# Pool rows, keys and two routings of the first token tile moved ahead of the second tile's work in a block with two expert layers

## The reference, cut to what matters

```python
def peer(h, wq, keys, u_tab, v_tab):          # per 128 tokens
    q = (hblk @ wq).reshape(128, 8, 2, 128)
    s = einsum('nhpd,hpkd->nhpk', q, keys)
    top_s, top_i = top_k(s, 16)                # two lists of 16 per head
    cand_s = top_s[:, :, 0, :, None] + top_s[:, :, 1, None, :]
    best_s, best_pos = top_k(cand_s, 16)       # idx: 16 experts per head
    gate = softmax(best_s)
    act = gelu(einsum('nd,nhkd->nhk', hblk, u_tab[idx]))
    return einsum('nhk,nhkd->nd', gate * act, v_tab[idx])

def mixer_pool(h, w_in, w_grp, scale, w_out):
    m = multiscale_pool(h @ w_in)              # a 256x256 band over tokens
    m = einsum('btgc,gce->btge', m, w_grp)
    return (m * scale) @ w_out
```

## Time and profile before

| what | value |
|---|---|
| median of 3 runs | 2202.29 us (2201.87 to 2202.67) |
| the profiled execution's own time | 2196.84 us |
| its span, first to last instruction | 2195.0 us |
| mean granted TensorE clock | 0.943 of full |
| busy: PE, DVE, ACT, POOL | 83%, 67%, 41%, 28% |
| read from HBM | 721.24 MB, 329 GB/s over the span |

### The profile page before, as it was taken

How to read it: one execution, slowest core, us unless ns; L and a number is a source line. 1 busy time by engine, 2 the same in 40 slices (tenths; PEclk the granted TensorE clock), 3 DMA queues, 4 the chain that set the end, 5 groups by cost and what they waited for, 6 DMA issues and landing times.

```text
span 2195.0 us, 21985 instructions
## 1 busy us (share of the span) xinstructions
PE 1816.2 (83%) x7101; PEld 1091.2 (50%) x7101; DVE 1466.8 (67%) x3029; ACT 897.5 (41%) x2357; POOL 618.9 (28%) x567
## 2 busy tenths in 40 slices
PE   4888999889978688888678787996798888877786
PEld 3757998788867344443323233354344443333222
DVE  6766956857776666767567767516666668677754
ACT  3446433524463333434334445312433344344433
POOL 1160000000000344434244343103354345443441
PEclk9889989989998899999899999998999899999999
DMA  9654758545563799999899999746899999999996
GB/s 367 265 198 145 262 196 306 177 171 211 202 220 116 316 371 418 418 421 421 338 402 421 421 421 421 319 172 256 362 416 419 419 421 421 421 421 421 421 422 251
DMA packets 114690, 723.76 MB, mean 330 GB/s; under 512 B 11504, under 2 KB 13344, under 8 KB 34064
## 3 DMA queue, kind: packets, MB, share of 16 engines
q0 software_dynamic: 74864, 540.30, 59.6%
q1 hardware_dynamic: 39712, 182.07, 22.7%
HBM read 721.24 MB, written 1.08 MB: 329 GB/s over the span
## 4 chain that ended last, share of the span: by engine, by line
PE 36%; DMA 31%; DVE 20%; ACT 6%; issue 5%; POOL 2%; SPq 0%; DVEq 0%; ACTq 0%; POOLq 0%
DMA X<-in_k_uv,EI 15%; PE PS L2129 14%; DMA Z<-in_k_uv,EI 9%; DMA W<-in_peer_wq 5%; PE PS L2106 5%; DVE junk L1809 4%; PE PS L1822 3%; PE PS L1823 3%; PE PS L1824 3%; DVE ACC L1429 3%; DVE WL L1445 3%; PE PS L1915 2%; ACT WH L999 1%; DMA W<-in_ada_w 1%; PE PS L2182 1%
## 5 line engine op out<-in xcount | busy, mean ns | idle before, releaser
L2129 PE MATMUL PS<-X,dg 128*128 128x512 f32 x1372 | 673.1, 626 | 176.2 <-ACT dg L999 175.4
L1809 DVE CUSTOM_DVE_ANT_0 junk<-H,X 128x1024 f32<-128x1024 f32 x343 | 419.6, 1223 | 254.0 <-DMA X<-in_k_uv,EI 247.0
L990 POOL DMA_INDIRECT X<-in_k_uv,EI x343 | 376.1, 1097 | 623.2 <-PE PS L2129 328.8
L2129 PEld LDWEIGHTS PS<-X,dg 128*128 128x128 f32 x1372 | 251.2, 195 | 553.3 <-ACT dg L999 345.6
L999 ACT ACTIVATE CF<-DOT 128x1 f32<-128x1 f32 x512 | 102.3, 200 | 588.7 <-DVE DOT L1809 588.2
L2129 PE MATMUL PS<-Z,dg 128*128 128x512 f32 x504 | 246.7, 622 | 38.3 <-ACT dg L999 38.2
L1809 DVE CUSTOM_DVE_ANT_0 junk<-H,Z 128x1024 f32<-128x1024 f32 x126 | 154.1, 1223 | 89.9 <-DMA Z<-in_k_uv,EI 86.7
L999 ACT ACTIVATE dg<-CP,CG 128x128 f32<-128x128 f32 x512 | 205.5, 401 | 17.3 <-PE PS L2129 0.6
L2129 PEld LDWEIGHTS PS<-Z,dg 128*128 128x128 f32 x504 | 92.6, 195 | 175.3 <-ACT dg L999 100.4
L1822 PE MATMUL PS<-XH,WH 128*128 128x256 f32 x592 | 176.2, 298 | 2.3 <-ACT XH L999 1.2
L990 POOL DMA_INDIRECT Z<-in_k_uv,EI x126 | 136.3, 1082 | 136.5 <-PE PS L2129 115.8
(11 more groups left out here) (312 smaller groups left out, 2626.8 us busy)
## 6 DMA issues: line engine op xcount, KB each, us to landing
W<-in_ada_w SPq DMA_DIRECT2D x56, 1024.0 KB, 5.1
Y<-in_ada_w SPq DMA_DIRECT2D x16, 1024.0 KB, 5.9
W<-in_k_win SPq DMA_DIRECT2D x16, 1024.0 KB, 5.1
W<-in_peer_wq SPq DMA_DIRECT2D x16, 1024.0 KB, 16.6
W<-in_k_ffi SPq DMA_DIRECT2D x13, 1024.0 KB, 5.4
Y<-in_k_ffi SPq DMA_DIRECT2D x9, 1024.0 KB, 4.9
W<-in_ffn_w_out SPq DMA_DIRECT2D x8, 1024.0 KB, 5.7
W<-in_ab_w_out SPq DMA_DIRECT2D x6, 1024.0 KB, 5.1
```

The lines of the kernel that those rows point to most:

```text
L990: e.indirect_dma_start(out=WS[k][:, :], out_offset=None, in_=I[f"k_uv{ly}"][:, :], in_offset=bass.IndirectOffsetOnAxis(ap=EI[t][:, j:j + 1 ...
L1809: e.tensor_tensor_reduce(junk, H[:, t, :], d[:, 0:D], 1.0, 0.0, ALU.mult, ALU.add, DOT[:, j:j + 1]).then_inc(v_dot, 1)
L2129: p = e.matmul(PS[:, 2 * t + q, :], dgb[n % 4][:, :], d[:, D + q * 512:D + (q + 1) * 512], start=(j == 0), stop=(j == 127))
```

## The change

What moves:

- Layer 1: the band, group and output products of the pool are split by tile. Tile 0's come first; tile 1's band follows, its `grp` and `po` stand behind the keys of heads 0 and 1, and its `rn`, `tt` and `h` behind the first experts. Layer 0: `rn` of tile 1 and `mod 9` change places with `tt` of tile 0.
- Both layers: chunks 0 to 3 of tile 0 come first, in banks 4 and 5, with the scores of heads 0 and 1 in bank 3. Heads 0 and 1 are routed one behind the other; tile 1's four chunks follow. The step without work at the end of each group goes.
- `experts` takes two steps behind each of the first 8 experts of tile 0.
- The pool's weight loads get eight slots of their own among the gather slots and stand ahead of everything else on SP; the gather ring has a new order. The gathers of layer 1 don't wait for the end of the pool any more, but for the slots they use.

```diff
-RING = list(range(2, 11)) + [13, 14, 15]
+RING = [9, 10, 4, 5, 3, 13, 2, 6, 14, 15, 7, 8]
...
-            b = bank(high)
+            b = 4 + i % 2 if (s4, hi) == (0, 128) else bank(high)
...
         if s4 == 0:
-            for lo in (0, 128):
-                for i in range(2):
-                    yield from chunk(i, lo, lo + 128)
-                if lo == 0:
-                    h00 = route(ly, 0, 0)
-                    next(h00)
-                    P("tt", ly, 1)
-                    yield from h00
-                    P("h", ly, 0)
-                    P("h", ly, 1)
-                    ready.add((ly, "h"))
+            for i in range(2):
+                yield from chunk(i, 0, 128)
+            h00 = route(ly, 0, 0)
+            next(h00)
+            for i in range(2, 4):
+                yield from chunk(i, 0, 128)
+            if ly:
+                for c in range(8):
+                    P("grp", c, 1, bank((1, 2)))
+                P("po", 1)
+            yield from h00
+            P("h", ly, 0)
+            ready.add((ly, "h"))
+            yield from route(ly, 0, 1)
+            if ly:
+                P("rn", ly, 1)
+                yield
+            P("tt", ly, 1)
+            yield
+            P("h", ly, 1)
+            for i in range(4):
+                yield from chunk(i, 128, 256)
+            return
...
-        yield
+        yield from route(ly, 0, 2 * s4 + 1)
...
             next(g, None)
+            if t == 0 and j < 8:
+                next(g)
...
     for ly in range(2):
-        P("rn", ly, 0)
-        if ly == 0:
+        if ly:
+            P("band", 0, 0, bank(low))
+            P("band", 1, 0, bank(low))
+            for c in range(0, 8, 2):
+                if c < 6:
+                    P("band", c + 2, 0, bank(low))
+                    P("band", c + 3, 0, bank(low))
+                P("grp", c, 0, bank(low))
+                P("grp", c + 1, 0, bank(low))
+            P("po", 0)
+            for c in range(8):
+                P("band", c, 1, bank((1, 2, 3)))
+            P("rn", ly, 0)
+        else:
+            P("ldq", ly, 0)
+            P("ldq", ly, 1)
+            P("ldk", ly)
+            P("rn", ly, 0)
+            P("rn", ly, 1)
             P("mod", 9, 0)
         P("tt", ly, 0)
-        P("rn", ly, 1)
...
-            P("ldp", 2)
-            P("ldp", 3)
+            for i in range(2, 10):
+                P("ldp", i)
+            P("ldq", 1, 0)
+            P("ldq", 1, 1)
+            P("ldk", 1)
...
-    rings = {"w": [0, 1, 2, 11, 12], "q": [0, 1], "p": [2, 6, 7, 8, 9, 10], "g": RING}
+    rings = {"w": [0, 1, 2, 11, 12], "q": [0, 1], "p": [3, 13, 14, 15, 7, 8, 9, 10], "g": RING}
...
-                    w.wait_ge(*arena(ly))
+                    w.wait_ge(p_part, 65)
+                    if ly and k in (4, 5):
+                        w.wait_ge(p_po, 1)
```

More of the change, by code:

```diff
@@ L417, in others @@
             yield from keys_part(ly, s4)
-            yield from route(ly, 0, 2 * s4 + 1)
         yield from between(ly)
@@ L498, in make_plan @@
             P("sc", 1)
[L499 to L507, removed]
     P("frn", 1)
@@ L545, in up @@
         return self.n
-NAME = {"xp": 3, "xt": 3, "mod": 2, "modp": 2, "gq": 3, "evac": 2, "rowp": 3, "rowa": 3, "pi": 4, "pie": 3, "band": 2, "grp": 2,
+NAME = {"xp": 3, "xt": 3, "mod": 2, "modp": 2, "gq": 3, "evac": 2, "rowp": 3, "rowa": 3, "pi": 4, "pie": 3, "band": 3, "grp": 3,
         "btp": 3, "bte": 3, "pqe": 5, "gate": 2}
@@ L850, in by_k, with scores @@
             return ap[:, :].rearrange("p (k n) -> p k n", k=k)
+        def scores(t, h):
+            return 3 if t == 0 and h < 2 else 7
         def arena(ly):
-            return (p_part, 65) if ly == 0 else (p_po, 1)
+            return (p_part, 65) if ly == 0 else (p_band, 16)
         def tt_done(name):
@@ L1291, in _ @@
                 elif kind == "band":
-                    c, b = a
-                    w.wait_ge(p_band, c + 1)
-                    act(mT[:, c, :], PS[:, b, 0:256], ACT.Copy).then_inc(a_band, 1)
+                    c, t, b = a
+                    w.wait_ge(p_band, 8 * t + c + 1)
+                    act(chunk(mT, c, t), PS[:, b, 0:128], ACT.Copy).then_inc(a_band, 1)
                 elif kind == "grp":
-                    c, b = a
-                    w.wait_ge(p_grp, c + 1)
-                    act(m2[:, c, :], PS[:, b, 0:256], ACT.Copy, scale=C2[:, c_psc + c:c_psc + c + 1]).then_inc(a_grp, 1)
+                    c, t, b = a
+                    w.wait_ge(p_grp, 8 * t + c + 1)
+                    act(chunk(m2, c, t), PS[:, b, 0:128], ACT.Copy, scale=C2[:, c_psc + c:c_psc + c + 1]).then_inc(a_grp, 1)
         @block.vector
@@ L2114, in _ @@
                     w.wait_ge(d_k, 16 * (ly + 1))
-                    take(7)
+                    b = scores(t, h)
+                    take(b)
                     for q in range(2):
                         c = 2 * h + q
-                        p = e.matmul(PS[:, 7, q * 128:(q + 1) * 128], chunk(PQ, c, t), KK[:, c, :], start=True, stop=True)
+                        p = e.matmul(PS[:, b, q * 128:(q + 1) * 128], chunk(PQ, c, t), KK[:, c, :], start=True, stop=True)
                     p.then_inc(p_rt, 1)
-                    free[7] = [(v_r7, nth("rt", ly, t, h, 2))]
+                    free[b] = [(v_r7, nth("rt", ly, t, h, 2))]
                 elif kind == "tail":
@@ L2154, in _ @@
                     take(b)
-                    for t in range(2):
-                        p = e.matmul(PS[:, b, 0:256], Z[:, t, c * 128:(c + 1) * 128], bd[:, c // 2, t, :], start=(t == 0),
-                                     stop=(t == 1))
+                    for i in range(2):
+                        p = e.matmul(PS[:, b, 0:128], Z[:, i, c * 128:(c + 1) * 128],
+                                     bd[:, c // 2, i, t * 128:(t + 1) * 128], start=(i == 0), stop=(i == 1))
                     p.then_inc(p_band, 1)
-                    free[b] = [(a_band, c + 1)]
+                    free[b] = [(a_band, 8 * t + c + 1)]
                 elif kind == "grp":
-                    c, b = a
+                    c, t, b = a
                     g = c // 2
```

45 lines of the change are left out of this document (21 added, 24 removed).

## The result

| | before | after |
|---|---|---|
| median, same chip | 2202.08 us (4 runs) | 2222.26 us (2218.56 to 2223.17, 4 runs) |
| profiled execution, its span | 2196.84, 2195.0 us | 2221.39, 2219.5 us |

The ratio is 1.0092 (95% interval 1.0074 to 1.0109): the change makes the kernel **20 us slower**. 2215 was forecast. On a second chip the changed kernel took 2225.21 us and the kernel before 2194.07 (ratio 1.0145, 1.0116 to 1.0174), 31 us more.

The account below looks back on a forecast made before the run. The DMA bounds the expert layers (512 gathers, 1275 us), with PE and DVE together as slow in the keys. Layer 0's +14.8 and layer 1's −1.5 sum to +13.3, told as 2215 us, range 2192 to 2228.

Parts of the forecast that it names:

- Slip of the first gather: Layer 0: rn of tile 1 and mod now precede tt, so the first gather starts 5.7 us later.
- Loads issued behind tile 1's last chunk, PE held 9.6: Layer 0, ahead of group 1: PE waits 9.6 us for query loads issued only then, holding tails and gathers behind it.
- Pause and lower clock: Layer 0, after PE's wait for loads: the DMA's rest lowers the granted clock to 0.50, costing 2.5 us (0 to 4).
- Rounds of 35.9, waits of 3.3: Keys: 35.9 us per 13 experts without the empty step; PE waits 3.3 us for second query loads in groups 2, 3.
- 92.9 gathers moved when the keys end: End of layer 0's keys (1002.2): 92.9 gathers moved against 101.4 before; the missing 8.5 cost 21.2 us, slip and pause included.
- The hole: Layer 0 at 1076 to 1096: DMA rest while tile 1's head 0 is late; earlier routing wins it, −10.2 us.
- Pool loads: End of layer 0: the early pool weight loads take DMA time from the last gathers, +3.8 us (bounds 0 to 8).
- Between the layers: Last tail of layer 0 to layer 1's first gather: splitting the pool by tile starts that gather 16.8 us earlier.
- Layer 1's keys: Layer 1, first gather to last tail: PE is held again by query loads; 15.3 us lost, leaving −1.5 for the layer.
- the prediction's own sign: Either layer: the prediction would be wrong if PE's wait for loads stayed under 5 us there.
- the keys aren't the limit: Keys of both layers: rounds go at the DMA's pace and 12 slots win the hold back; −8 us, 2194; chance 0.19.
- The rival of even shares: Query loads beside gathers: a load gets half the DMA, the four 3.3 us waits go; 2203, no change; chance 0.15.

Follow-up runs that it names:

- the fastest: Changed kernel with layer 0's keys in old order, two steps behind experts 116 to 127, six workless steps and 29 tails a group in layer 1: 2182.15 us.
- the kernel before without its hole: Kernel before, with two steps behind each of experts 116 to 127 of tile 0 in layer 0: 2187.16 us, ratio 0.996.
- The kernel with 29 tails: Changed kernel with six workless steps ahead of group 1, three more per later group, two steps for experts 112 to 127 of layer 0: 2190.88 us.
- eleven steps: 29-tail kernel with eleven workless steps for six ahead of group 1, layer 0's rn of tile 1 behind tt, double steps for experts 104 to 127: 2195.03 us.
- two kernels with later pool loads: Changed kernel with pool loads 4 to 9 held back until tail 251, or until tail 255: 2224.17 and 2227.14 us.
- layer 0's old order: Changed kernel with layer 0 up to its last routing in the order of the kernel before, early pool loads and ring kept: 2212.0 us.

## Why the prediction was right, and where it was off

The sign and the likeliest case came out: 2215 forecast, 2222 measured on that chip, and 13.3 of forecast loss stand against 24.5 between the profiled executions and 20.2 between the medians. The mechanism is the one forecast, PE held by query loads and too few tails in the keys. Its size in layer 0 was taken too small, and in layer 1 two terms were off that made up for each other.

- **Slip of the first gather, +5.7.** From the products ahead of layer 0 to the first gather the rows give 27.5 us with the change. With rn of tile 1 behind tt they give 21.5 (three kernels) or 23.5 (before and the fastest), so it costs 4 to 6. It doesn't show in the span, because the stages ahead of layer 0 ended 4.2 us earlier in this execution; their end lies anywhere between 695.6 and 703.1 in the executions of kernels with this order. Right.
- **Loads issued behind tile 1's last chunk, PE held 9.6.** The trace has 9.65 (8.60 on the second chip), until 776.97 and not 781.1. Right in size; but the runs show that its length is a poor measure of its cost. With four tails more ahead of it, 8.09 us of it were left and 11 us won.
- **Pause and lower clock, 2.5.** The clock's part is right: the granted clock was 0.50 (the lower of its two levels) at 776 to 782, PE's first product behind the hold took 3.75 us for 8 matmuls (1.99 at full clock), and the next tail 2.78 for 1.88, 2.7 in all. But the scores of head 2 came 18.1 us behind the hold, where 13.8 + 2.5 were forecast. The sum left out that ACT empties the first chunk before it makes the next diagonal, for which PE waited 1.32 us (until 786.35).
- **Rounds of 35.9, waits of 3.3.** 795.06 to 830.92 is 35.9; the waits were 2.90 and 2.25. The first two stretches from a group's scores to the next's took 77.1 and 74.6 us, forecast 75.1 each. Right.
- **92.9 gathers moved when the keys end.** This is the step that was mis-sized. Counted from each kernel's own first gather, 282 us on, the queue had moved 102.6 gathers before and 91.9 after: 10.7 fewer, 26.6 us (9.5 fewer on the second chip). The forecast's 21.2 less the slip are 15.5, so some 11 us were missed. Head 2's scores came 71.9 us behind the first gather, where 68.5 were forecast (1.6 for loads issued later, 1.8 behind the hold). By head 7's scores it was 261.8 for 254.6, so the groups took another 3.8 more. And 2.1 gathers were in flight at the end (94 issued, 91.9 moved) where 1.1 were taken, 2.5 us. That makes 9.7; the other 1.4 us stay open.
- **The hole, −10.2.** −8.3 (medians) and −8.7 (layer 0 of the profiled execution) in the kernel before without it. A little large.
- **Pool loads, +3.8.** 5.1 with only them, 6.7 in the fastest version. The forecast let 2.0 MB pass ahead of the last gather. 4.88 moved beside the last gathers, but holding six of the eight loads back gave only 1.1 us at the last gather, so the price is near that of the first two loads. "At most 8" held.
- **Between the layers, −16.8.** −14.5 and −15.9. Right: from the last tail's end (1439.76) to the start of rn (1484.90) the pool took 45.1, as forecast, with rn, turning, chunks and routing behind. In the chunks PE ran part of the time at the lower clock, so the first gather came 2 us later than forecast.
- **Layer 1's keys, 15.3 lost again.** 16.3 and 19.8. Right in the sum, in part by luck. The hold there was forecast at 6.5 us and measured 2.06 and 0.60. The loads of group 1 were issued 52.3 us behind the first gather and not 49.7, during chunks in which a tail came only every 7 us (1557.33, 1564.11), and a tail stood ahead of group 1. Head 2's scores then came 72.2 us behind the first gather, forecast 71.7, and 92.9 gathers had moved 276.5 us on, forecast 93.9. By the prediction's own sign ("under 5 us in a layer") the waits of layer 1 pass only if those of all groups are added, 6.3 us.

The rival "the keys aren't the limit" is half right, and that is the most useful miss. "In the keys PE and DVE together are as slow as the DMA" holds for 13 tails a round, but it isn't a limit: a round has room for one or two tails more at 0.4 us each (58 tails in 154.2 us, 52 in 151.7). The change took the empty step away and gave the heads a lead of 16 to 31 experts in layer 0. The kernel with 29 tails has leads of 10 to 18 there and keeps the DMA busy; the rest of the lead is tails not done. The rival of even shares is out: the waits of 2.25 to 2.90 us for the second load came as forecast from its small share. The rule of the Trainium skill (DMA: Bandwidth & Descriptors, Queues, rings and completion order) on turns between queues by whole packets was not put to a run of its own. The earlier trace rows agree with it if its packets are those of the profile: 439 of the gathers and 429 of the loads, of unequal size, so the bytes are not even.

## What to carry to other kernels

When a stream of transfers is fed by work that shares engines with something else, count how many transfers each group of the other work lets through, and compare that with the time of the group: here a group of 26 took 75.9 us, in which the DMA could have moved two loads and 28.5 gathers, so it lost 6 us each time, and 29 lost none. A lead that is larger than the buffers can use is paid for in exactly that; take it back as steps without work. Don't take back so much that a routing comes late while the queue is already short: eleven steps gave no gain over six. A gain ahead of such a stretch (15 us here) stays only if the stretch is kept full.

## What the runs showed of the hardware

- The last transfer of a stream ends with its slowest DMA engine: with 10.49 MB queued the rate fell from 404 to 82 GB/s in some 3 us and then ran at 82 to 20 for 5.6 us. With no load beside the gathers it fell in the same way (399 to 20 GB/s, in the kernel before without its hole). Taking 2.8 MB of other loads away from the last gather gave 1.1 us, not 6.6.
- Two loads that were issued 2.5 us apart beside a full queue of gathers landed 16.0 and 25.9 us after their issue, and the same 16.1 and 26.1 in the changed kernel, whatever followed them.
- Where PE and DVE set the pace, a lower granted clock costs time. The program of layer 1 is the same in five of the executions above (the changed kernel twice, its two kernels with later pool loads, and layer 0's old order). It took 697.7, 699.8, 701.2, 703.7 and 709.1 us, at mean granted clocks of 0.98, 0.97, 0.97, 0.96 and 0.96; PE was busy 565.8, 566.0, 568.7, 577.9 and 577.8 us with the same matmuls, and DVE 465.4 to 465.6. In a stretch at 421 GB/s a window at 0.83 costs nothing that shows (1086 to 1096 in the kernel before without its hole, 419 GB/s).
